# The first half of an FFN down projection as seven-product block pairs, its output in hT, block sums of u kept in DRAM meanwhile, and an end that runs by row tiles

## The reference, cut to what matters

```
D_MODEL = 1024; D_FF = 2816
def swiglu(x, w_gu, w_down):
    gate, up = jnp.split(x @ w_gu, 2, axis=-1)
    return (jax.nn.silu(gate) * up) @ w_down
def trunk(...):
    for layer in range(2):
        g = norms[layer]
        u = rmsnorm(h, g[0])
        mix, ... = mixer(u, ...)                    # layer 0 or layer 1
        h = h + rmsnorm(mix, g[1])
        h = h + rmsnorm(swiglu(rmsnorm(h, g[2]), w_gu[layer], w_down[layer]), g[3])
    return h, ...                                   # rows of h, and the layers' states
```

## Time and profile before

| | us |
|---|---|
| three runs | 2697.49, 2699.34, 2700.47 |
| the profiled execution | 2699.14 |
| its span on the core | 2697.5 |
| TensorE busy in the span | 2619.7 |
| VectorE, ScalarE, GpSimd busy | 1248.5, 1020.5, 447.4 |

### The profile page before, as it was taken

How to read it: one execution, slowest core, us unless ns; L and a number is a source line. 1 busy time by engine, 2 the same in 40 slices (tenths; PEclk the granted TensorE clock), 3 DMA queues, 4 the chain that set the end, 5 groups by cost and what they waited for, 6 DMA issues and landing times.

```text
span 2697.5 us, 49450 instructions
## 1 busy us (share of the span) xinstructions
PE 2619.7 (97%) x20215; PEld 1873.4 (69%) x20215; DVE 1248.5 (46%) x2064; ACT 1020.5 (38%) x1886; POOL 447.4 (17%) x513
## 2 busy tenths in 40 slices
PE   8999899999999999999999999999999999999997
PEld 5666666656688668886566766667657886788765
DVE  5555533335754214444754444344467441144444
ACT  4454332224444214433443332324355441234332
POOL 4000023222023002211101010110101210122121
PEclk9999999999999999999999999999999999999998
DMA  7211269771211311124435242322411122011442
GB/s 250 63 40 42 86 221 343 242 247 51 77 64 32 81 53 63 48 88 149 121 88 92 40 111 52 95 77 74 151 72 50 62 60 59 32 64 48 145 129 86
DMA packets 257660, 266.15 MB, mean 99 GB/s; under 512 B 10668, under 2 KB 217810, under 8 KB 256796
## 3 DMA queue, kind: packets, MB, share of 16 engines
q1 hardware_dynamic: 231772, 166.10, 22.0%
q0 software_dynamic: 25088, 94.79, 9.9%
q10 hardware_dynamic: 576, 2.10, 0.2%
HBM read 227.45 MB, written 35.50 MB: 97 GB/s over the span
## 4 chain that ended last, share of the span: by engine, by line
PE 90%; DVE 5%; ACT 2%; issue 2%; DMA 0%; POOL 0%; DVEq 0%; SPq 0%; ACTq 0%; POOLq 0%
PE ps L371 48%; PE ps L1116 25%; PE ps L1920 2%; PE ps L1908 1%; PE ps L1606 1%; PE ps L1959 1%; PE ps L1685 1%; PE ps L2454 1%; PE ps L2434 1%; PE ps L2468 1%; DVE arena L872 1%; DVE hT L876 1%; PE ps L2490 1%; PE ps L2477 1%; PE ps L1671 1%
## 5 line engine op out<-in xcount | busy, mean ns | idle before, releaser
L371 PE MATMUL ps<-u,w_split 128*128 128x352 f16 (+1 forms) x4752 | 750.6, 314 | 9.8 <-DVE u L736 5.9
L371 PEld LDWEIGHTS ps<-u,w_split 128*128 128x128 f16 (+1 forms) x4752 | 461.8, 98 | 258.8 <-issue 20.3
L371 PE MATMUL ps<-arena,w_split 128*128 128x352 f16 x3663 | 560.6, 313 | 3.7 <-DVE w_split L344 1.5
L371 PEld LDWEIGHTS ps<-arena,w_split 128*128 128x128 f16 x3663 | 357.6, 98 | 200.7 <-issue 9.4
L1116 PE MATMUL ps<-hT,w_split 128*128 128x264 f16 x3456 | 400.6, 276 | 3.2 <-ACT arena L1156 3.2
L1116 PEld LDWEIGHTS ps<-hT,w_split 128*128 128x128 f16 x3456 | 337.8, 98 | 54.8 <-issue 2.1
L344 DVE SCALAR_TENSOR_TENSOR w_split<-w_raw,w_split 128x1024 f16<-128x1024 f32 (+2 forms) x133 | 184.5, 1388 | 295.8 <-ACT w_split L328 295.2
L1116 PE MATMUL ps<-u,w_split 128*128 128x264 f16 x2592 | 303.4, 276 | 0.0
L1116 PEld LDWEIGHTS ps<-u,w_split 128*128 128x128 f16 x2592 | 253.6, 98 | 38.3
L328 ACT ACTIVATE w_split<-w_raw 128x1024 f16<-128x1024 f32 (+2 forms) x133 | 155.5, 1171 | 136.7 <-PE ps L371 97.8
L342 DVE SCALAR_TENSOR_TENSOR w_split<-arena,w_split 128x512 f16<-128x512 f32 x126 | 85.9, 724 | 103.9 <-ACT w_split L322 103.9
(11 more groups left out here) (398 smaller groups left out, 2979.4 us busy)
## 6 DMA issues: line engine op xcount, KB each, us to landing
w_raw<-in_w_down SPq DMA_DIRECT2D x58, 704.0 KB, 4.7
w_raw<-in_w_in SPq DMA_DIRECT2D x56, 512.0 KB, 7.8
arena<-in_w_gu SPq DMA_DIRECT2D x18, 1024.0 KB, 5.2
w_raw<-in_w_gu SPq DMA_DIRECT2D x18, 1024.0 KB, 5.1
hT<-in_cache_k SPq DMA_DIRECT2D x64, 256.0 KB, 4.3
hT<-in_cache_k POOLq DMA_DIRECT2D x64, 256.0 KB, 4.5
hT<-in_cache_v SPq DMA_DIRECT2D x64, 256.0 KB, 5.1
hT<-in_cache_v POOLq DMA_DIRECT2D x64, 256.0 KB, 5.5
```

What stands on the lines that cost most here:

```text
L371: ins = pe.matmul(ps[0:m, bank, 0:GW], split_of(v, wp)[:, k * w + col * P:k * w + col * P + m], x[:, xp, k0 + k, cols(g)], start=(k == 0 a ...
```

## The change

1. **Down projection of half 0.** add_products is given four more "pairs" of kind "down", appended behind the eight gate and up pairs. The 11 tiles of hid are cut in tiles 0 to 2 (a tail) and 3 to 10. Two output tiles (i, i+1) times tiles 3 to 10 are seven products M1 to M7 (24 matmuls of 264 columns each, even tiles of hid against odd ones), the tail is four plain products P11, P12, P21, P22 (18 matmuls of 264 columns each), which accumulate into banks of M2, M3, M4 or into banks 6 and 7. That replaces 792 matmuls of 352 columns in each layer. Each pair loads its weights with one DMA of 1024 KB and one of 384 KB; GpSimd makes the four weight sums for it as for the others.
2. **Block sums of hid.** After each of the four up pairs of half 0, new t2 jobs make T1 to T4 of hid: VectorE does dve_t2_far (one subtraction of 1056 columns), then the older jobs (dve_low), then dve_t2_near (two subtractions of 528), all before the next evacuation; ScalarE casts twice 1056 columns one unit later; VectorE makes two low parts (1056 columns each) another unit later. They go to t_hid, rows 11 to 18.
3. **y in hT.** The down pairs write y to hT, half 1's down projection adds to it there, and the saved h comes back to ybuf instead of hT. dve_chain for these norms reads y from hT and h from ybuf.
4. **Block sums of u.** t_of (in hT) is saved to a new DRAM tensor t_spill early in half 0 and read back into rows 11 to 18 by one DMA of GpSimd's queue, issued when M4 of the last down pair is done. M6 of half 1 waits for it.
5. **The end.** In the last group ScalarE scales y by the gain after each square; the eighth square is summed by a second TensorE matmul instead of GpSimd; VectorE works by row tiles (8, 5, 6, 7) with two operations each; transposes, copies and output DMAs follow by tile, the last tile's copy shared by ScalarE and VectorE.

```diff
+            def finish(p):
+                return [(p, m) for m in (("M4", "P21", "P22", "M3", "P12") if todo[p][0] == "down" else ("M4", "M3"))]
+            for p, (kind, i) in enumerate(todo):
+                if kind == "down" and todo[p - 1][0] != "down":
+                    order += finish(p - 1) + [(p, m) for m in ("P11", "M1", "M2", "M6", "M5", "M7")]
+                elif kind == "down" and p == len(todo) - 1:
+                    order += [(p, "M1")] + finish(p - 1) + [(p, m) for m in ("M6", "M5", "M7", "P11", "M4", "P21", "M2", "M3",
+                                                                             "P12", "P22")]
+                else:
+                    order += [(p, "M1")] + (finish(p - 1) if p else []) + ([(p, "P11")] if kind == "down" else [])
+                    order += [(p, m) for m in ("M2", "M6", "M5", "M7")]
...
         def pe_down(pe, n):
+            if name == "P11" and extra["first"]:
+                pe.wait_ge(hid_ready, hid_made[layer, 0, 2, 2])
+            if name == "M2" and extra["first"]:
+                pe.wait_ge(hid_ready, hid_made[layer, 0, KF - 1, 0])
+            if name == "M6" and extra["first"]:
+                pe.wait_ge(hid_ready, t2_cast[layer])
+            for s_ in range(2):
+                for k in range(3 if name[0] == "P" else 4):
+                    if name == "M1" and extra["first"] and not s_:
+                        pe.wait_ge(hid_ready, hid_made[layer, 0, 3 + 2 * k, 0])
...
         def pe_product(pe, n):
+            if name == "M6" and half_:
+                pe.wait_ge(restored, (16, 160)[layer])
...
+        def act_t2(act, n):
+            act.wait_ge(evac["dve"], turn + 1)
+            act.activation(t_hid[:, 2:4, 0, k, :], t24, ACT.Copy).then_inc(hid_hi, 1)
+            act.activation(t_hid[:, 0:2, 0, k, :], t13, ACT.Copy).then_inc(hid_hi, 1)
+        def dve_t2_far(dve, n):
+            dve.wait_ge(evac["dve"], turn - 1)
+            dve.tensor_tensor(t13, arena[:, 21:23, T // 2:T], two(21), ALU.subtract).then_inc(evac["dve"], 1)
...
         def pool_ffn(pool, layer):
+            for p, (load, first, base) in enumerate(pool_jobs[layer]):
+                if p == 2:
+                    pool.wait_ge(hid_ready, t_cast[layer])
+                    pool.dma_start(t_spill, hT[:, :, :]).then_inc(spilled, 16)
+                if p == PAIRS0:
+                    pool.wait_ge(unit_done, last_t[layer] + 1)
+                    pool.wait_ge(spilled, (64, 176)[layer])
+                    pool.dma_start(rows(11, 8), t_spill).then_inc(restored, 16)
...
-                pool.dma_start(hT[:, :, cols(g)], spill[:, :, cols(g)]).then_inc(restored, 16)
+                pool.dma_start(ybuf[:, :, cols(g)], spill[:, :, cols(g)]).then_inc(restored, 16)
...
         def dve_ffn(dve, units_):
             for n in units_:
+                if n in t2_jobs:
+                    dve_t2_far(dve, n)
                 for job in later:
                     job()
                 later.clear()
+                if n in t2_jobs:
+                    dve_t2_near(dve, n)
                 splits_lo(dve, n)
...
+        def end_tile(dve, chain, tt):
+            a, b = max(tt * P, 2 * GW), min(tt * P + P, T)
+            dve.wait_ge(y_gained, KD)
+            y, old = hT[:, :, a:b], ybuf[:, :, a:b]
+            chain.link(dve.tensor_tensor(y, y, r, ALU.mult))
+            dve.tensor_tensor(y, y, old, ALU.add).then_inc(h_ready, 1)
+        END_TILES = (8, 5, 6, 7)
```

More of the change, by code:

```diff
@@ L501, in add_products @@
                 assert n == at[p, name]
-                bank = {"M2": 6, "M5": 4, "M3": 4}.get(name, 2 * (place["pair"] + p & 1))
-                by = "act" if name in ("M1", "M6", "M7") or name == "M4" and kind == "gate" else "dve" if name != "M5" else None
-                flush()
+                bank = {"M2": 6, "M5": 4, "M3": 4, "P11": 6, "P22": 6, "P12": 4}.get(name, 2 * (place["pair"] + p & 1))
+                if kind == "down":
+                    by = {"M1": "act", "M6": "act", "M7": "act", "P21": "act", "M2": "dve", "P12": "dve", "P22": "dve"}.get(name)
+                else:
+                    by = "act" if name in ("M1", "M6", "M7") or name == "M4" and kind == "gate" else "dve" if name != "M5" else None
+                flush()
+                ahead = order[n - start - 1] if n > start else None
+                if downs and ahead and ahead[1] == "M3" and todo[ahead[0]][0] == "up":
+                    t2_jobs[n] = layer, ahead[0] // 2, turns["dve"] + 1, (cast(), cast())
+                    t2_his[n + 1] = t2_jobs[n]
+                    turns["dve"] += 2
+                    t2_cast[layer] = casts["n"]
+                    read_turn["row", 0] = read_turn["row", 1] = casts["n"]
                 turn = 0
@@ L508, in add_products @@
                     turn = turns[by]
-                if name in ("M1", "M2", "M5"):
+                if name in ("P21", "P12") or kind == "down" and name == "M2":
+                    events = []
+                elif name in ("M1", "M2", "M5", "P11", "P22"):
                     events = sorted({holder[b] for b in (bank, bank + 1) if b in holder})
@@ L530, in add_products @@
                     read_turn["v1"] = turn
-                if name == "M3":
+                if name == ("P12" if kind == "down" else "M3"):
                     read_turn["v2"] = turn
+                if name == "P21":
+                    y_done[layer, i // 2] = [turn]
+                if name in ("P12", "P22"):
+                    y_done[layer, i // 2].append(turn)
+                if kind == "down" and name == "M4":
+                    last_t[layer] = n
                 if mn and kind == "gate":
@@ new lines, in dve_down @@
+        def dve_down(dve, n):
+            (kind, layer, half_, i, name, _, _), extra, mn = products[n]
+            if name not in ("M2", "M7", "P22", "P12"):
+                return
+            dve.wait_ge(unit_done, n + 1)
+            x, out, with_ = pair_psum(n), y_block(i, 1, 1), y_block(i, 1, 1)
+            if name in ("M2", "P12"):
+                drained(dve, extra["m1" if name == "M2" else "m6"])
+                dve.wait_ge(spilled, (64, 176)[layer])
+                out, with_ = y_block(i, 0, int(name == "P12")), keep[name == "P12"]
+            elif name == "M7":
+                drained(dve, n)
+                x = ps[:, 4:6, 0:HW]
+            else:
+                dve.wait_ge(evac["dve"], sum_turn[extra["m7"]])
+            dve.scalar_tensor_tensor(out, x, 1 / WS, with_, ALU.mult, ALU.add).then_inc(evac["dve"], 1)
```

243 lines of the change are left out of this document (166 added, 77 removed).

## The result

The changed kernel takes 2703.89 us (median of 12 runs, 2700.89 to 2707.43), the kernel before 2699.57 on the same chip (12 runs, 2696.89 to 2702.39): a ratio of 1.0017, 95% interval 1.0009 to 1.0024. That is 4.3 us more where 11.3 us less were forecast, and outside the predicted range. The profiled execution took 2703.19 us with a span of 2701.6, against a span of 2697.5 before.

A forecast was written before the change was run, and what follows sets the result against it. TensorE, busy 97% of the span, was taken as the bound. 2699.14 - 21.4 (matmuls) + 5.2 (up pairs) + 8.0 (hand-over) + 0.3 (sums of u) - 3.3 (end) = 2688.0 us, range 2679 to 2695.

The forecast's parts named there:

- Matmul time, and that the rest of the other engines is hidden: Down stage of half 0: matmul time falls 21.4 us in all; other engines' work costs 0, far bound 22 us.
- Work behind every up pair: Behind the first three up pairs, VectorE's t2 work stalls TensorE 0.87 us before M7: +5.2 us, bounds 0 and +10.
- The hand-over: Start of the first down pair: stalls of 2.4 us for tile 9's low part and 1.6 before M6, +8.0 in all.
- Nothing in the new stage idles long enough to differ from the waits of today: Down stage of half 0: the granted clock stays 1.00, the full 2.4 GHz, as in the profile before.
- Block sums of u: Half 1: the read-back lands within the 16.9 us before M6; +0.3 us in all, bounds 0 and +8.
- falls into it: Layer 0: a weight load of 1024 KB falls into the read-back's time; +0.3 us taken for it.
- (c): Rival: late read-back of the sums of u, before M6 of half 1; 2699 us if 22.5, 2706 if 26; chance 0.12.
- (a): Rival: GpSimd's sums for the next pair hold VectorE's new low parts, six places at 1 us: 2694 us; chance 0.12.
- (b): Rival: the t2 jobs and the hand-over cost next to nothing, 2675 us; chance 0.14.
- (d): Rival: the change doesn't thin the down stage's matmuls; excluded by the counts, no chance given.
- The end: End of the kernel: GpSimd's last add, update chain and copies shorten, output DMA stays; -3.3 us, bounds -1 and -5.

## Why the prediction was wrong

**Matmul time, and that the rest of the other engines is hidden:** right but for one wait. 960 matmuls at 112.5 ns, -21.4 us; no product of the stage waits for an evacuation but P22. That is a late evacuation, which this term had put at nothing and at 0.7 us for its far bound; it cost 15.5.

**Work behind every up pair:** right path, size a half too large, 0.87 forecast for 0.58 each. Counted from the start of M6, the M2 evacuation moved from 789.52 - 786.98 = 2.54 us to 790.65 - 786.69 = 3.96, 1.42 for the 1.7 that I took; less the slack of 0.83 that is 0.59. The run with the subtractions later shows the path.

**The hand-over:** right, 4.15 for 4.0 a layer, with the two waits where they were forecast. What was missing is that a wait can be followed by matmuls at half clock: 1.5 us in layer 1. "Nothing in the new stage idles long enough to differ from the waits of today" was wrong on the prediction's own numbers, 2.4 us beside 0.79.

**Block sums of u:** this step failed: +0.3 us forecast, +18.2 measured. Weights that "are issued a whole pair ahead" holds for the down pairs, of which it was said; for the load behind them, that of half 1's first block pair, nothing was asked. I looked at one victim, the read-back, and asked whether it lands before M6. In layer 1 it does, after 13.3 us, within the 16.9. In layer 0 it took 21.0, 4.1 beyond them, and M6 didn't wait only because P22 had held TensorE; that this sign came out right there is luck. With the order mended it lands after 14.9. The weight load "falls into it" was there, but priced only for what it does to the read-back. What the read-back does to a load of four times fewer bytes in packets over thirty times smaller (10.9 us), what SP's queue holds ahead of this load (the two w_in loads, in layer 0 alone, which the change itself had put there), and what stands behind its splits on ScalarE and VectorE were not asked. With the order mended 1.7 of the 18.2 us stay, with the read-back nearly gone 7.5, with it held back 11.1.

**The rivals:** (c) had the right trigger, the read-back, and the right side, but the wrong waiter: M6 never waits in the changed kernel. (a) VectorE held by GpSimd is real and costs nothing in the changed kernel: at 793.53 two low parts (line 1301) took 4.33 us beside GpSimd's sums of up to 2.17, and 2.43 without them at 906.37, and TensorE didn't wait for either. The Trainium skill (SBUF — State Buffer, Who interferes with whom) says that both have to take turns when each reads SBUF; the trace agrees. Once the order is mended, contention does reach TensorE, with about 1.1 us before M2 of half 1. (b) and (d) didn't come.

**The end:** too small. -5.3 by the two traces (-4.6 to -5.0 in the run of its own) for -3.3: 3.9 came from the chain up to the last evacuation, where 3.3 was forecast, 1.4 from the output DMA and the rest, which I had left as it was.

With +0.3 in place of +18.2 and no slow stretch the measured terms give 2699.14 - 21.4 + 3.5 + 8.3 + 0.3 - 5.3 = 2684.5; the runs with the order mended, with a wait of 1.6 us and slow stretches in them, were at 2685.4 to 2691.6.

Open: which part of the late load's 14.2 us without a read-back is the w_in load ahead of it and which is its own was told apart only roughly, by the sizes of the packets: half a KB, as w_in's, until about 1000 us, five after the issue, and about 1 KB from then on. Nor is it known why the clock falls behind a wait of 2.3 us in some executions and not in others.

## What to carry to other kernels

When a big transfer is added, list every transfer in flight beside it and follow each to its waiter; the new transfer may be on time and still be the cause. For each load in that list read when its queue lets it be issued, and for each split or copy that waits for a load, what stands behind it in its engine's order: a load that is late costs what is queued behind its consumer. Price a wait on TensorE together with the matmuls behind it: the one of 2.3 us here cost 1.5 us more in one layer, the one of 15.5 us cost 2.5 more.

## What the runs showed of the hardware

- A 1024 KB load in packets of about 1 KB takes 5.2 us alone. Beside a 4224 KB transfer in packets of some 30 KB it took 10.5 (the save, at 760 us of the changed kernel), 11.8 (the read-back, with the order mended) and 7.4 (the read-back held). It took 14.2 behind a 512 KB load in packets of half a KB, which alone takes 8.2 itself, and 26.8 with both.
- TensorE stood at granted clock 0.50 behind a wait of 2.3 us in layer 1 (39 matmuls in 6.08 us), and at 1.00 behind the same wait in layer 0 (4.56 us). Of the six profiles with this wait, slow matmuls followed it in layer 1 in three (the changed kernel, the order mended, the w_in loads later) and in layer 0 in none. Behind waits of 1.3 and 0.4 us the pace stayed full.
- The time of the runs of one kernel roughly follows the mean granted clock: 2700.9 us at 0.990 to 2707.4 at 0.987 for the changed kernel.
